# A fused three-block kernel: the scan's head pairs start 4 ticks later and stand 4 ticks apart, and one more group's SiLU runs whole on ScalarE

## The reference, cut to what matters

```python
zxbcdt = rms_norm(x, ln_g) @ in_w                       # z, x/B/C, dt
xbc = jax.nn.silu(causal_dwconv(xbc, conv_w, conv_b))   # 4 taps along the sequence
dt = jax.nn.softplus(dt + dt_bias); a = dt * (-jnp.exp(a_log))
y = ssd_chunked(xs32 * dt[..., None], a, bm, cm)        # 32 heads in 4 groups, chunks of 128
y = y + xs32 * d_skip[:, None]
y = y * jax.nn.silu(z)                                  # gate, then a norm by group
```

## Time and profile before

| | us |
|---|---|
| median of 3 runs (2403.49 to 2405.24) | 2404.54 |
| the profiled execution, its own time | 2402.46 |
| its span in the profile | 2400.7 |
| TensorE busy in the span | 2376.7 |
| mean granted TensorE clock (share of full) | 0.998 |

### The profile page before, as it was taken

One profiled execution on the slowest core, in us unless ns is written; L12 is line 12 of the kernel. 1 busy time (PEld: TensorE's weight loads), 2 busy tenths in 40 slices (PEclk: granted clock), 3 DMA queues, 4 the chain that ended last, 5 costly groups with the idle time before them and its releaser, 6 DMA issues.

```text
span 2400.7 us, 29668 instructions
## 1 busy us (share of the span) xinstructions
PE 2376.7 (99%) x11556; PEld 1930.8 (80%) x11556; DVE 1403.3 (58%) x2203; ACT 1052.5 (44%) x1803; POOL 370.8 (15%) x297
## 2 busy tenths in 40 slices
PE   8999999999999999999999999999999999999999
PEld 6777888888888877788888877787788877888887
DVE  6778776763665678766456557534555445443343
ACT  6654564442444677644234334324443334322223
POOL 0352252210111000121012100001211001110011
PEclk9999999999999999999999999999999999999999
DMA  4632223223223221232332332231243322223222
GB/s 164 110 92 79 81 74 101 88 86 109 96 82 127 72 71 54 75 102 94 98 102 87 99 131 72 78 102 61 68 132 128 114 97 88 88 95 99 105 78 90
DMA packets 74844, 226.19 MB, mean 94 GB/s; under 512 B 8144, under 2 KB 12368, under 8 KB 74576
## 3 DMA queue, kind: packets, MB, share of 16 engines
q1 hardware_dynamic: 70272, 215.90, 27.5%
q10 hardware_dynamic: 4432, 8.39, 2.0%
HBM read 215.87 MB, written 8.39 MB: 93 GB/s over the span
## 4 chain that ended last, share of the span: by engine, by line
PE 62%; DVE 1%; issue 0%; ACT 0%; POOLq 0%; POOL 0%; DVEq 0%
PE bank L1189 60%; PE bank L1193 1%; DVE t L2073 0%; ACT t L1595 0%; DVE t L2070 0%; DVE t L2081 0%; DVE t L2077 0%; ACT t L1598 0%; DVE t L2563 0%; POOLq L2862 0%; POOL t L2641 0%; DVEq L2862 0%; DVE t L2409 0%; DVE t L2078 0%; DVE t L2569 0%
## 5 line engine op out<-in xcount | busy, mean ns | idle before, releaser
L1189 PE MATMUL bank<-t 128*128 128x512 f32 (+4 forms) x11130 | 2352.3, 377 | 16.7 <-DVE t L2073 7.8
L1189 PEld LDWEIGHTS bank<-t 128*128 128x128 f32 (+2 forms) x11130 | 1888.0, 185 | 450.2 <-issue 80.0
L1595 ACT ACTIVATE t<-t 128x1024 fp32r<-128x1024 f32 (+6 forms) x634 | 539.3, 861 | 645.4 <-PE bank L1189 276.1
L2070 DVE TENSOR_TENSOR t<-t 128x1024 fp32r<-128x1024 f32 (+6 forms) x686 | 624.1, 920 | 260.6 <-ACT t L1595 254.5
L2641 POOL TENSOR_TENSOR t<-t 128x512 f32<-128x512 f32 (+4 forms) x217 | 329.0, 1523 | 1543.9 <-ACT t L1598 558.7
L1598 ACT ACTIVATE t<-t 128x512 f32<-128x512 f32 (+6 forms) x610 | 367.4, 616 | 450.3 <-DVE t L2070 301.2
L2070 DVE TENSOR_TENSOR t<-bank,t 128x512 f32<-128x512 f32 (+4 forms) x412 | 276.0, 674 | 451.9 <-PE bank L1189 441.5
L2073 DVE SCALAR_TENSOR_TENSOR t<-t 128x512 f32<-128x512 f32 (+4 forms) x493 | 364.0, 748 | 103.4 <-ACT t L1598 63.8
L1595 ACT ACTIVATE t<-bank 128x512 f32<-128x512 f32 (+4 forms) x151 | 72.2, 498 | 167.0 <-PE bank L1193 145.2
L2644 POOL TENSOR_SCALAR t<-t 128x128 f32<-128x128 f32 (+3 forms) x64 | 41.1, 649 | 476.8 <-ACT t L1595 246.1
L2073 DVE SCALAR_TENSOR_TENSOR t<-bank,t 128x512 f32<-128x512 f32 x56 | 38.5, 687 | 67.3 <-PE bank L1189 67.3
(11 more groups left out here) (30 smaller groups left out, 52.9 us busy)
## 6 DMA issues: line engine op xcount, KB each, us to landing
t<-in_w SPq DMA_DIRECT2D x304, 512.0 KB, 3.3
t<-in_w SPq DMA_DIRECT2D x48, 384.0 KB, 3.0
t<-in_w SPq DMA_DIRECT2D x56, 320.0 KB, 2.9
t<-in_w SPq DMA_DIRECT2D x28, 256.0 KB, 2.7
tab<-t ACTq DMA_DIRECT2D x1, 2560.0 KB
t<-in_x SPq DMA_DIRECT2D x8, 256.0 KB, 5.3
t<-tab SPq DMA_DIRECT2D x8, 256.0 KB, 3.9
spill<-t ACTq DMA_DIRECT2D x1, 2048.0 KB, 8.7
```

The costliest lines, as they stand in the source:

```text
L1189: return eng.matmul(out, lhs, rhs, start=start, stop=stop, skip_group_check=loose)
L1595: return eng.activation(out, in_, ACT.Copy, scale=scale)
L2070: return eng.tensor_tensor(out, a, b, o)
```

## The change

The first pair of group 0 starts when `stb` is 14 ticks old, not 10 (the other groups stay at 10), and in all groups each next pair starts 4 ticks later, not 3. [...] The branch that was added for z's tiles is never taken, as `silu_whole` asks for kind "in".

```diff
-                self.once("pair", (g, p), lambda g=g, p=p: self.past("stb", g, 10)
-                          and (p == 0 or self.past("pair", (g, p - 1), 3)),
+                self.once("pair", (g, p), lambda g=g, p=p: self.past("stb", g, 10 if g else 14)
+                          and (p == 0 or self.past("pair", (g, p - 1), 4)),
...
     def silu_whole(self, key):
-        return key[:2] == ("in", 0) or key in (("in", 1, 0), ("in", 1, 1), ("in", 1, 2))
+        kind, g, i = key
+        return kind == "in" and (g in (0, 2) or g == 1 and i < 4)
...
+            if i == 0 and g == 2:
+                load_set(SILU_AND_TANH)
...
         for g, p in at("pair", T - 1):
             n = 4 * g + p
-            if n == 0:
-                eng.add_instruction(mybir.InstLoadActFuncSet(name=eng.bass.get_next_instruction_name(), engine=eng.engine,
-                                                             act_func_set_id=EXP_AND_TANH))
+            if n in (0, 8):
+                load_set(EXP_AND_TANH)
```

More of the change, by code:

```diff
@@ L30 @@
 N_MAIN = 3
-EXP_AND_TANH, LN_AND_EXP = 0, 6
+EXP_AND_TANH, LN_AND_EXP, SILU_AND_TANH = 0, 6, 18
 def t5_bucket(n):
@@ L805 @@
     "hi", "lo", "sq", "add_d", "add_p", "pow",
-    "pad", "tap0", "tap", "tanh", "silu", "silu_first", "dtx", "neg", "absn", "ealog", "expn", "ln1", "dt", "adt", "cs", "tail",
+    "pad", "tap0", "tap", "tanh", "silu", "silu_whole", "dtx", "neg", "absn", "ealog", "expn", "ln1", "dt", "adt", "cs", "tail",
     "ds", "csd", "csh", "xds", "stm", "sub", "edec", "gm", "yadd", "gate", "yn",
@@ L1079, in activated @@
     def activated(self, key):
-        return self.sig["silu_first" if self.silu_whole(key) else "silu"].at(*key)
+        return self.sig["silu_whole" if self.silu_whole(key) else "silu"].at(*key)
     def silu_whole(self, key):
-        return key[:2] == ("in", 0) or key in (("in", 1, 0), ("in", 1, 1), ("in", 1, 2))
+        kind, g, i = key
+        return kind == "in" and (g in (0, 2) or g == 1 and i < 4)
     def u_before(self, key):
@@ L1598, in func, with load_set @@
         return eng.activation(out, in_, f, bias=bias, scale=scale, accum_out=accum)
+    def load_set(i):
+        eng.add_instruction(mybir.InstLoadActFuncSet(name=eng.bass.get_next_instruction_name(), engine=eng.engine,
+                                                     act_func_set_id=i))
     def split(u):
@@ L1697, in ssm @@
             if K.silu_whole(key):
-                func(ACT.Silu, dst, dst, scale=2.0).then_inc(*sig["silu_first"].up(*key))
+                func(ACT.Silu, dst, dst, scale=2.0).then_inc(*sig["silu_whole"].up(*key))
                 continue
@@ L1705, in ssm @@
             w.wait_ge(*K.activated(old))
-            func(ACT.Tanh, buf.us[plan.u_n[key] % 3][:, 4:S + 4], buf.ZT[g % 2][:, i, :]).then_inc(*sig["tanh"].up(key))
+            z = buf.ZT[g % 2][:, i, :]
+            if K.silu_whole(key):
+                func(ACT.Silu, z, z, scale=2.0).then_inc(*sig["silu_whole"].up(*key))
+                continue
+            func(ACT.Tanh, buf.us[plan.u_n[key] % 3][:, 4:S + 4], z).then_inc(*sig["tanh"].up(key))
         for _ in at("once", T):
@@ L1715, in ssm @@
             w.wait_ge(*sig["absn"].at())
-            eng.add_instruction(mybir.InstLoadActFuncSet(name=eng.bass.get_next_instruction_name(), engine=eng.engine,
-                                                         act_func_set_id=LN_AND_EXP))
+            load_set(LN_AND_EXP)
             func(ACT.Exp, buf.ctot[:, 0:32], pc("alog", 0, 32)).then_inc(*sig["ealog"].up())
@@ L1825, in diff @@
             func(ACT.Exp, buf.l4[:, 2:4], buf.l4[:, 0:2]).then_inc(*sig["lam5"].up())
-            eng.add_instruction(mybir.InstLoadActFuncSet(name=eng.bass.get_next_instruction_name(), engine=eng.engine, act_func_set_id=LN_AND_EXP))
+            load_set(LN_AND_EXP)
         for key in at("hn", T - 1):
```

## The result

| | before | after |
|---|---|---|
| median of 6 runs each, us | 2404.01 (2403.37 to 2405.24) | 2423.93 (2423.66 to 2425.64) |
| span of the profiled execution, us | 2400.7 | 2422.3 |
| mean granted TensorE clock | 0.998 | 0.995 |

The change makes the kernel slower: ratio 1.0083, 95% interval 1.007 to 1.0096, 19.9 us by the medians. The forecast was 2415.2, with a range up to 2422. So the sign was right, and the loss nearly twice what was worked out.

The account below looks back on a forecast made before the run. TensorE, busy 2376.7 of 2400.7 us, was taken as the bound. 6.8 + 6.1 - 2.2 = 10.7 us on the profiled 2402.46 made 2413.2, and 2.08 us to the median made 2415.2; range 2403 to 2422.

Parts of the forecast that it names:

- part 1: First pairs of group 0: old stall goes, but Exps behind a late weight load hold bank 3; +6.8 us.
- part 2: Last pairs of group 1: table loads delay ScalarE, VectorE and GpSimd, so `by` waits; +6.1 us.
- SiLU wait at 192.59: Group 2: TensorE's 1.33 us wait for a VectorE SiLU multiply goes, as ScalarE does the silus.
- `gm` wait at 248.42: Group 2: TensorE's 0.92 us wait for GpSimd goes, as pairs get 8.0 us instead of 6.66.
- last pair of group 3: Group 3: last part of Y ready 4.1 us later, still ahead of its use; 0, bound 0.5 us.
- then 0.7, three taps 2.31 to 12.4: Group 1's second pair: VectorE's taps take 2.31 us ahead of the `bo` multiply, costing `by` 3.2 us.
- rival E: Worse than forecast: prices low clock behind the wait at group 1's last pairs at 2.3 us, 2417.5 us; chance 0.13.
- the waits of 1.2 and 1.7 us at the third and fourth pair: Group 1: `by` of these pairs waits for GpSimd's second `gm`, losing 1.2 and 1.7 us.
- the seven set loads: Group 1's last pairs: ScalarE table loads of 1.28 us each, ahead of work TensorE soon needs; bound 9.0 us.
- part 3: Later groups: group 2's SiLU and `gm` waits go, group 3 costs 0; -2.2 us.
- D: Faster: neither new wait, and the stall at 96.5 us goes with its low clock; 2397.0 us, chance 0.07.
- A stall at each switch of sets: ScalarE's table loads: a stall at every switch; chance 0.03, within that of rival E.

Follow-up runs that it names:

- experiment 5: Changed kernel with ScalarE issuing the two table writes at ticks 57 and 69, not 33 and 53: 2441.01 us, ratio 1.0157.
- experiment 4: Changed kernel with the split of the weights for tick 61 on, and its low part, two ticks later: 2419.78 us, ratio 1.0071.
- experiment 6: Kernel before with only the first pair of group 0 moved to age 14: 2414.53 us against 2402.86.
- experiment 9: Changed kernel with GpSimd's `gm` multiplies of pair (1, 1) on one column, not 512: 2421.78 us.
- experiment 1: Changed kernel without its SiLU part, so only the pairs' ticks differ from before: 2422.39 us against 2403.64.
- experiment 7: Kernel before with only the distance of the pairs changed from 3 to 4 ticks: 2416.66 us against 2403.14.
- experiment 10: Changed kernel without its SiLU part and with VectorE's multiply of `bo` one tick earlier: 2425.52 us against 2403.14.
- experiment 11: The kernel of experiment 10 with VectorE's normalisation multiplies of Y0 and taps of group 2's first three tiles on one column: 2420.70 us, ratio 1.0071.
- experiment 3: Changed kernel with group 3's pairs 3 ticks apart as before: 2418.21 us, ratio 1.0064.
- experiment 13: Kernel before with the set load three ticks earlier, first pair's Exps ahead of their tick's Tanh, and two weight splits behind Exps: 2400.19 us against 2403.14.
- experiment 2: Kernel before with only the SiLU part and its two set loads, pairs at their old ticks: 2403.97 us against 2403.64.
- experiment 8: Changed kernel with VectorE's multiply of `bo` one tick earlier, ahead of taps and low parts: 2426.98 us, ratio 1.01.

## Why the prediction was wrong

The sum was 10.7 us and 19.9 came. Term by term, with the idle times and half-clock stretches of the profiled execution:

| term | forecast | measured | from |
|---|---|---|---|
| part 1 | +6.8 | +6.2 | 1.68 + 9.48 - 4.17 idle; 1.7 - 2.5 low clock |
| part 2 | +6.1 | +8.1 | 4.63 + 0.55 idle; 2.9 low clock |
| SiLU wait at 192.59 | -1.3 | -1.3 | gone |
| `gm` wait at 248.42 | -0.9 | +0.8 | 1.34 + 0.34 - 0.92 |
| last pair of group 3 | 0 | +5.3 | 3.71 idle; 1.6 low clock |
| elsewhere | 0 | +1.7 | low clock without a wait, at 1427 us |

These are 20.8 us. The span grew by 21.6, of which 0.4 lie before 70 us; 0.4 us are not attributed.

**Part 1 was right**, in each step that has a row: when the load lands, what the chain behind it takes, which bank is missed. Experiment 5 shows the table write as the cause, experiment 4 the split's place, experiment 6 that the later first pair brings the wait by itself. Only the low clock behind it was sized 0.6 us too high (2.3 for 1.7): the clock was low from 102.8 us on, and most of that passed while TensorE was idle.

**Part 2 was right in its chain, and wrong in two sizes and in its cause.** The step "then 0.7, three taps 2.31 to 12.4" took a duration measured with GpSimd idle; beside `gm` the taps take 3.94 (experiment 9). And the sum left out the low clock behind a wait of this length, which stood only in rival E: 4.63 us brought 2.9 us of it. In return the waits of 1.2 and 1.7 us at the third and fourth pair were 0 and 0.55. The cause that I named, the seven set loads, is half of the 4.63 us at most. Experiments 1, 6 and 7 have waits of 2.3 to 3.6 us at that place with none of them, and experiments 10 and 11 point to VectorE's stream as a whole.

**The step that failed**, the largest that the sum lacks, is in part 3: "by the plan it is then still a tick ahead of its use, so I take 0, with 0.5 us as its bound". It asked who needs the result of the moved pair, and not what stands around the moved pair on VectorE. When a step of the plan moves, each of its instructions takes a new place in the queue of its engine: here the multiply of `bo` came behind the normalisation of Y2. It is 5.7 us by experiment 3, and without it the time is 2418.2, inside the range. "The pairs of group 2 have 8.0 us for what had 6.66: the 0.92 us at 248.42 go" failed too. The wait became 1.34 and 0.34 us at 263.55 and 279.25, and experiment 7 has the same two with only the spacing changed. In the rows of the kernel after, the Exps of that pair stand behind a split, where before they stood ahead of one, since units of weights come every 4 ticks as the pairs now do; that this is the cause is argued, not shown.

**The rivals.** D, faster, was right on one thing: that the first pairs' stall could be had for less. It took other moves than this change makes (experiment 13). E, worse, priced the low clock behind part 2's wait at 2.3 us and so came to 2417.5; that clock came, with 2.9 us. A stall at each switch of sets, which has 0.03 of the chances, is shown by no run and is no term of the sum: the table load at 105.22 us takes 1.28 us and the next instruction begins at 106.51, as before at 92.13 and 93.43.

**Open.** Experiment 7 has 6 us of idle time in group 0 where there were 4.2 before, in four waits; no experiment took them apart. The clock falls near 1427 us in the changed kernel and at 1406 to 1429 us in experiments 2, 7 and 11, and not in the kernel before; no run shows why. 0.4 us of the profiled execution have no place.

## What to carry to other kernels

When a plan's number moves a group of instructions, list for every moved instruction what now stands ahead of it on its own engine, at every place where the number acts, and not only at the first; here the last of sixteen pairs cost nearly as much as the first (5.3 and 6.2 us). Where a bank passes through several readers on one busy engine, moving one reader only chooses the next that is late (in experiment 10 the addition at 187.18 us, with a wait of 2.57 us behind it): look at the stream's backlog before looking at its order. And price a wait of some microseconds on TensorE with the half clock behind it; here waits of 9.48, 4.63 and 3.71 us had 1.7, 2.9 and 1.6 us of it.

## What the runs showed of the hardware that was not expected

- Operations of VectorE took longer beside GpSimd's: three taps 3.94 us beside `gm` and 2.31 us with `gm` on one column (experiment 9), and a low part of 128x512 1.78 us at 359.70 us beside GpSimd, where 0.68 us is its time at 344.60 us in the kernel before. GpSimd's own three operations at that pair of group 1 took between 3.97 us (experiment 10) and 4.93 us (experiment 1).
- Two writes of 2560 and 1536 KB from 8 partitions, issued at 104.09 and 127.13 us, were done at 192.27 us, while loads of 512 KB issued beside the first of them in the kernels before and after take 17.7 us instead of 3.2 (experiment 5).
- A wait's length doesn't say whether the clock falls. It stayed at 1.00 behind 3.09 us (experiment 8, 207.88 us) and 2.00 us (experiment 4, 103.83 us), and was 0.50 behind 1.86 us (experiment 4, 117.74 us), behind 1.56 us (experiment 1, 225.72 us) and behind each wait of over 3.1 us but the one at the start of the kernel. In the kernel after it was 0.50 at 1427 us with no wait from 1395 us on:

```profile
1427.15:1430.55 3.40, 3.40 (x12) 2.70 (x11) 1.58 (x5) 0.60 (x1) 0.00 (x0) 0.50 0.23 64
```
